# Banded attention scores: one mask product per PSUM bank ahead of the scores, and scores alternating between row halves and banks

## What is computed

```python
kb, vb = band(k), band(v)                  # previous block and own block, 256 keys
s = jnp.einsum('bnqkgd,bnjkd->bnkgqj', qb, kb) * (dh ** -0.5)
diff = W + qi - kj
in_win = (diff >= 0) & (diff < W)          # and no keys before token 0
s = jnp.where(mask[None, :, None, None], s, -jnp.inf)
p = jax.nn.softmax(jnp.concatenate([s, sink], axis=-1), axis=-1)[..., :2 * W]
o = jnp.einsum('bnkgqj,bnjkd->bnqkgd', p, vb)
```

## Time and profile before

| | us |
|---|---|
| median of 3 runs | 1267.82 |
| lowest, highest | 1262.52, 1271.57 |
| the profiled execution | 1269.59 |
| its span in the profile | 1267.9 |
| TensorE busy in it | 1190.8 |

### The profile page before, as it was taken

How to read it: one execution, slowest core, us unless ns; L and a number is a source line. 1 busy time by engine, 2 the same in 40 slices (tenths; PEclk the granted TensorE clock), 3 DMA queues, 4 the chain that set the end, 5 groups by cost and what they waited for, 6 DMA issues and landing times.

```text
span 1267.9 us, 17480 instructions
## 1 busy us (share of the span) xinstructions
PE 1190.8 (94%) x5132; PEld 653.3 (52%) x5132; DVE 696.0 (55%) x1627; ACT 326.3 (26%) x731; POOL 46.4 (4%) x89
## 2 busy tenths in 40 slices
PE   6999999999698999999979999999996899999996
PEld 3754555556593444444457545555565744444443
DVE  3345564467674555555542365545767745555554
ACT  4215231024312222222142152211242222222221
POOL 7000000000006000000000000000000000000000
PEclk9999998999798999999989999989997999999999
DMA  9140023400405999999541300245004089999981
GB/s 284 33 132 1 1 67 123 177 34 1 199 1 179 401 422 422 422 422 422 201 143 32 102 1 1 67 133 199 1 2 199 1 316 404 421 422 422 422 374 67
DMA packets 52549, 243.14 MB, mean 192 GB/s; under 512 B 8320, under 2 KB 18848, under 8 KB 27392
## 3 DMA queue, kind: packets, MB, share of 16 engines
q1 hardware_dynamic: 49344, 240.40, 48.0%
q0 software_dynamic: 2560, 1.89, 0.9%
q10 hardware_dynamic: 576, 0.02, 0.0%
HBM read 240.19 MB, written 2.10 MB: 191 GB/s over the span
## 4 chain that ended last, share of the span: by engine, by line
PE 85%; DVE 7%; issue 2%; ACT 2%; DMA 1%; DVEq 1%; ACTq 1%; SPq 0%
PE ps L2519 18%; PE ps L2124 10%; PE ps L2552 9%; PE ps L2344 8%; PE ps L2116 7%; PE ps L2503 6%; PE ps L2504 4%; PE ps L2094 4%; PE ps L2145 4%; PE ps L2489 2%; PE ps L2392 2%; PE ps L2186 2%; PE ps L2488 2%; DMA X<-in_x 1%; PE ps L2194 1%
## 5 line engine op out<-in xcount | busy, mean ns | idle before, releaser
L2519 PE MATMUL ps<-wgu,xw 128*64 128x512 f32 x1024 | 228.8, 600 | 7.8 <-ACTq L1179 6.7
L1958 DVE TENSOR_TENSOR X<-ps,X 128x512 f32<-128x512 f32 x256 | 156.0, 682 | 10.9 <-issue 9.0
L2124 PE MATMUL ps<-hT,ring 128*128 128x512 f32 x352 | 158.4, 606 | 0.0
L2519 PEld LDWEIGHTS ps<-wgu,xw 128*64 128x64 f32 x1024 | 76.8, 138 | 153.9 <-issue 153.9
L2552 PE MATMUL ps<-wdn,hhT 128*64 128x512 f32 x512 | 120.3, 613 | 2.8 <-ACTq L1197 2.8
L2344 PE MATMUL ps<-ring,yT 128*128 128x512 f32 x256 | 119.5, 616 | 0.4 <-DVE X L1356 0.4
L2503 PE MATMUL ps<-yhi,Wt 128*128 128x512 f32 x256 | 114.1, 446 | 3.7 <-DVEq L1242 3.7
L2124 PEld LDWEIGHTS ps<-hT,ring 128*128 128x128 f32 x352 | 67.4, 196 | 78.2 <-issue 78.2
L2504 PE MATMUL ps<-ylo,Wt 128*128 128x512 f32 x256 | 101.1, 395 | 0.0
L1976 DVE SCALAR_TENSOR_TENSOR ylo<-ps,ws,yhi 128x512 fp32r<-128x512 f32 x64 | 48.1, 751 | 74.1 <-ACTq L1207 74.1
L1965 DVE TENSOR_TENSOR hh<-ps,silu 128x256 f32<-128x256 f32 x32 | 13.6, 425 | 124.6 <-ACTq L1185 124.6
(11 more groups left out here) (367 smaller groups left out, 1505.0 us busy)
## 6 DMA issues: line engine op xcount, KB each, us to landing
wgu<-in_w_gate SPq DMA_DIRECT2D x64, 1024.0 KB, 9.0
wgu<-in_w_up SPq DMA_DIRECT2D x64, 1024.0 KB, 11.1
wdn<-in_w_down SPq DMA_DIRECT2D x64, 1024.0 KB, 10.9
ring<-in_w_in SPq DMA_DIRECT2D x8, 1024.0 KB, 6.6
ring<-in_w_mix_out SPq DMA_DIRECT2D x12, 512.0 KB, 6.0
w_kv<-in_xa_w_kv SPq DMA_DIRECT2D x2, 2048.0 KB, 10.0
ring<-in_w_in SPq DMA_DIRECT2D x2, 2048.0 KB, 17.6
ring<-in_w_in SPq DMA_DIRECT2D x2, 1536.0 KB, 16.6
```

Of the source, the lines that this page charges most:

```text
L1958: tt(xh, bank, xh, ALU.add).then_inc(mfreed((what, n)), 1)
L2124: last = mm(bank, w[:, c, c0:c0 + P], hT[:, c, :], start=c == 0, stop=c == KD - 1)
L2519: last = mm(bank[r], xw[:, c, r], wgu[2 * parity + j][:, :, c, :], start=c == 0, stop=c == KD - 1)
```

## The change

The two masks become the halves of one tile, `mask16`. In a window unit TensorE first opens both banks: for each, one product of the identity with the mask repeated for both heads (`start=True`, 256 or 512 columns). Then come the four products of queries and keys, which add to it, in the order bank 0, bank 1, bank 0, bank 1, that is row half 0, 1, 0, 1. The cross units take the same order of products, without masks. The latent units are as before. At POOL's setup one memset takes the place of two.

```diff
-        causal16 = small("causal16", [P, P], BF16)
-        before16 = small("before16", [P, P], BF16)
+        mask16 = small("mask16", [P, 2, P], BF16)
+        before16, causal16 = mask16[:, 0], mask16[:, 1]
...
-                for k in range(2):
-                    bank = bank_of(l, ("S", unit, k))
-                    per = len(heads) // 2
-                    for i, (pair, h) in enumerate(heads[per * k:per * (k + 1)]):
-                        s = bank[:, 512 // per * i:512 // per * i + L]
...
-                        last = mm(s, lhs, rhs, start=True, stop=kind == "xa")
-                        if kind == "swa" and nk == 2:
-                            mm(s[:, 0:P], ident16[:], before16[:], start=False, stop=False)
-                        if kind != "xa":
-                            last = mm(s[:, L - P:L], ident16[:], causal16[:], start=False, stop=True)
-                    last.then_inc(filled(("S", unit, k)), 1)
+                per = len(heads) // 2
+                banks = [None, None]
+
+                def opened_bank(k):
+                    banks[k] = bank_of(l, ("S", unit, k))
+                    if kind == "swa":
+                        mask = mask16[:, 2 - nk:].rearrange("p b n -> p (b n)").unsqueeze(1).to_broadcast([P, per, L])
+                        mm(banks[k].rearrange("p (a n) -> p a n", a=per)[:, :, 0:L], ident16[:], mask,
+                           start=True, stop=False)
+
+                def scored(k, i):
+                    pair, h = heads[per * k + i]
+                    s = banks[k][:, 512 // per * i:512 // per * i + L]
...
+                    elif kind == "swa":
+                        last = mm(s, qTC[rows, pair, q], kTC[rows, (t + 1) * P - L:(t + 1) * P],
+                                  start=False, stop=i == per - 1)
+                    else:
+                        last = mm(s, qTx[rows, t % 2, pair, :], kTx[rows, pair, 0:L], start=True, stop=True)
+                    if i == per - 1:
+                        last.then_inc(filled(("S", unit, k)), 1)
...
+                    opened_bank(0)
+                    opened_bank(1)
+                    for i in range(per):
+                        for k in range(2):
+                            scored(k, i)
```

More of the change, by code:

```diff
@@ L770, in _ @@
             pool.iota(slot_0[:], pattern=[[0, 1]], base=0, channel_multiplier=1, allow_small_or_imprecise_dtypes=True)
-            pool.memset(causal16[:], 0.0)
-            pool.memset(before16[:], 0.0)
+            pool.memset(mask16[:], 0.0)
             pool.memset(earlier16[:], 1.0)
@@ L778, in _ @@
             pool.drain()
-            pool.affine_select(out=causal16[:], in_=causal16[:], compare_op=ALU.is_ge, fill=NEG,
+            pool.affine_select(out=causal16, in_=causal16, compare_op=ALU.is_ge, fill=NEG,
                                base=0, pattern=[[-1, P]], channel_multiplier=1)
-            pool.affine_select(out=before16[:], in_=before16[:], compare_op=ALU.is_gt, fill=NEG,
+            pool.affine_select(out=before16, in_=before16, compare_op=ALU.is_gt, fill=NEG,
                                base=0, pattern=[[1, P]], channel_multiplier=-1)
@@ new lines, in score @@
+                per = len(heads) // 2
[9 more added lines that the diff above has]
+                    s = banks[k][:, 512 // per * i:512 // per * i + L]
+                    rows = slice(h * HD, (h + 1) * HD)
+                    if kind == "mla":
+                        last = mm(s, qTA[0:QK, 2 * pair + h, q], kTA[0:QK, 2 * pair + h, 0:L], start=True, stop=False)
+                        last = mm(s[:, L - P:L], ident16[:], causal16, start=False, stop=True)
+                    elif kind == "swa":
[5 more added lines that the diff above has]
+                        last.then_inc(filled(("S", unit, k)), 1)
@@ L2152, in turn @@
+                if kind == "mla":
+                    for k in range(2):
+                        opened_bank(k)
+                        for i in range(per):
+                            scored(k, i)
+                else:
+                    opened_bank(0)
+                    opened_bank(1)
+                    for i in range(per):
+                        for k in range(2):
+                            scored(k, i)
             def turn(l, unit, u, pr):
```

## The result

The changed kernel takes 1259.16 us (median of 8 runs, 1252.81 to 1262.92) beside 1269.67 (8 runs, 1262.52 to 1271.57) for the kernel before. The ratio is 0.9928, with a 95% interval of 0.9906 to 0.995: 9 us less, 6 to 12. In a later comparison it was 0.991 [0.9893, 0.9927]. The forecast was 1256.0, in a range of 1251 to 1262. The profiled execution took 1260.16 us.

A forecast was written before the change was run, and what follows sets the result against it. TensorE was taken to bound the kernel, with 85% of the chain. Window units gain 1.35 and 1.78 us each, of which 5.9 a layer arrives; 11.8 off the median 1267.82 gives 1256.0, range 1251 to 1262.

The forecast's parts named there:

- A unit of 256 keys, 1.60; tile 0's, 0.96: Window scores on TensorE: 256-key unit 1.60 us instead of 3.28, gain 1.78; tile 0's 0.96, gain 1.35.
- The halves overlap when they add to a mask in the bank: Window scores: the two row halves run side by side, four products in 1.07 us as in the cross scores.
- rival without overlap: Window scores: halves do not overlap, unit 2.47 us, gain 0.9 a unit, 7.2 in all, 1260.6 us; chance 0.10.
- How much arrives: Unit 0 to first latent unit: DVE is late next at unit 3, PE waits 0.8 us, 5.9 us a layer arrives.
- Bank waits and cross scores, 0: Waiting for bank 1 before all products costs 0; the cross scores' new order gains 0, staying at 1.07 us.
- The sum, -11.8: Whole kernel: 5.9 us a layer, 11.8 in two, off the median 1267.82 gives 1256.0; chance 0.68.
- PE's clock falls more often: Rival: PE's new 0.8 us wait a layer brings one more clock fall, 3.4 us in all, 1259.4; chance 0.14.

The follow-up runs named there:

- the two runs with another order: The change with score products in bank order behind both masks: 1255.94 us; the change with each bank's mask just ahead of its two products: 1264.69 us.
- Keys first: The change, with VectorE copying the latent keys (kTA) ahead of three convolution instructions: 1246.65 us, 0.9836 to the kernel before; again 1249.09 us, 0.9854.
- Both reorderings on DVE: The change, with latent keys copied ahead of the convolution and unit 2's weights normalised before head_rstd, both on VectorE: 1248.14 us, 0.9848 to the kernel before.
- Filling the wait: The change, with ten unneeded mask products a layer before TensorE waits for the latent keys: 1247.14 us, 0.9843 to the kernel before.

## Why the prediction was right

*A unit of 256 keys, 1.60; tile 0's, 0.96.* Right: 1.60 and 1.59, and 0.96. The terms are right too: masks 0.215 each, products 1.06 to 1.08 entry to entry.

*The halves overlap when they add to a mask in the bank.* Right, shown by the two runs with another order. The prediction left open whether the order of the products matters; it doesn't. Its picture of the unit is not whole: the overlap is half of the 1.78 us, and the other half is three changes of height at 0.29 us, which its sum held within the measured 3.28 without naming them. Its rival without overlap, gain 0.9, is that half.

*How much arrives.* Right. DVE had 0.30 us left before unit 1's maximum, as worked out. Unit 2 found DVE and ACT free. At unit 3 DVE was late next: its maximum follows the normalisation at once (0.26 instead of 1.25), and PE waits. The wait is 0.60 us where 0.8 was worked out (PE was ready at 125.77, not 125.52). From unit 0's start the first latent unit comes 5.88 us earlier in layer 0 and 5.91 in layer 1 (5.9 forecast).

*Bank waits and cross scores, 0.* Right: no wait stands before unit 1's masks or between them and its products (the chain goes from the one to the other without a gap), and the cross scores changed alone give 1.0001.

*The sum, -11.8.* Right: 5.88 + 5.91 in the profile, 5.87 + 5.91 in that of the repeat. In the times it arrives within their spread. The medians give -10.5 in the first comparison and -12.1 in the second (1268.52 to 1256.46), the mean spans of all 13 executions -10.4, and 11.8 lies inside both intervals (6 to 12, and 9 to 14). Of the 3.2 us by which 1259.16 misses 1256.0, 1.9 are the starting point: the forecast subtracts from 1267.82, a median of three runs, and before gave 1269.67 here.

*PE's clock falls more often.* The 0.60 us wait brings no fall; the clock is 1.00 over all of 99 to 138 us, so this rival did not come about where it was placed. Whether the change makes the clock fall for longer elsewhere stays open. In the means it has 90 us of half clock (13 executions) against before's 87, worth some 1.5 us at half a us each, which would be what is missing in the mean spans. But the two comparisons of the change, 91 and 88, lie as far apart as that.

*My expectations of the runs* failed in six places. The kernel with a mask for each bank took 2.75 us a unit where I had 2.55 (I priced a change of height and back at 0.20; it is 0.29), and its ratio, 0.9966, lies just above my 0.994 to 0.996. The change again showed 88 us of half clock, not 90 or more. Keys first came out at 0.9836, and 0.9854 again, where I first had 0.986 to 0.990. Both reorderings on DVE did not add up. Filling the wait gained 9 us, not 3 to 5, of which the profiles show 5 behind the waits. And the same filler gained nothing clear of noise in the kernel before, where I had 8 to 9, carried over from that one result.

## What to carry to other kernels

Here products on one half of the rows ran beside those of the other half, each half adding to a bank of its own, in whatever order they were issued, as long as no full-height instruction stood between them. So put masks and other full-height additions first or last, one for each bank: it buys the overlap, and it saves the changes of height, which were worth as much. When such a change is worked out, follow it until another engine is late next, as here DVE at unit 3, and take the sum there. Where the clock falls behind a wait of TensorE, try first whether the awaited copy can be issued earlier on its engine; moving that one copy on VectorE gave 7 to 10 us, nearly as much as the whole change and about twice the wait itself. Filling the wait instead gave 9 us in one kernel and nothing clear of noise in the other. And count half clock only where TensorE is busy: in a wait it costs nothing.

## What was not expected of the hardware

- TensorE took products of one row half ahead of earlier products of the other half: eight passes issued as four and four took 1.08 us, four passes of one half alone 1.06.
- Changing from 128-row to 64-row products and back costs 0.29 us together (0.10 before the first pass, 0.19 behind the last); the masks for each bank paid it twice, the kernel before four times a unit.
- Ten unneeded products (2.33 us) in a wait of 2.42 kept the clock at 1.00 behind it, and the kernel was 9 us faster (1255.1 to 1246.0 in mean span). In the kernel before the same filler gave 0.9987 [0.9966, 1.0008].
- How long a fall of the clock lasts differs between executions of the same kernel: the same 32 products behind the same wait of 3.23 us took 9.84 us in one and 8.78 in another.
- With five waits filled or removed in each layer 36 us of half clock are left of 88, and the kernel takes 0.9783 of the time before. Of the 43.5 us taken away by the last four only 9.7 reached the end; in the traces 19 of 50 lay in time in which TensorE was idle.
